# Recurrence gates as fp32 products in four quarters of the array, in place of three products on split operands

## The reference

```python
def lru_coeffs(xc, wa, ba, wx, bx, lam):
    xh = xc.reshape(B_, N, LRU_HEADS, LRU_HD)            # 8 heads of 64
    r = sigmoid(einsum('bnhi,hij->bnhj', xh, wa) + ba)
    i = sigmoid(einsum('bnhi,hij->bnhj', xh, wx) + bx)
    log_a = (-LRU_C * r) * softplus(-lam)
    a = exp(log_a)
    b = sqrt(-expm1(2.0 * log_a)) * (i * xc)
```

## Time and profile before

| | us |
|---|---|
| median of 3 runs | 797.6 |
| the profiled execution | 795.27 |
| its span, first to last instruction | 793.2 |
| TensorE busy | 740.0 |
| VectorE busy | 534.0 |
| ScalarE busy | 449.4 |
| GpSimd busy | 273.5 |
| mean granted clock of TensorE | 0.966 |

### The profile page before, as it was taken

The page is one execution under the profiler, slowest core; times in us unless marked ns, Lnnn a source line. Parts: engine busy times, 40 slices in busy tenths (PEclk is TensorE's granted clock), DMA queues, the critical chain, the costliest instruction groups (busy, mean ns, idle before and its releaser), DMA issues.

```text
span 793.2 us, 9934 instructions
## 1 busy us (share of the span) xinstructions
PE 740.0 (93%) x3468; PEld 602.5 (76%) x3468; DVE 534.0 (67%) x811; ACT 449.4 (57%) x743; POOL 273.5 (34%) x321
## 2 busy tenths in 40 slices
PE   3876989999999998999998999989999999999997
PEld 1575767888888877888887887758787888888885
DVE  4377654759997789788996655776645665766532
ACT  4266652798786975887984982334535133534311
POOL 0022335243435254224433456223211145443421
PEclk9596999999999998999999999989999999999999
DMA  9998003334355245344453134344458667967531
GB/s 363 347 324 242 27 28 107 93 97 117 116 181 173 64 157 173 99 126 137 163 167 112 58 104 142 98 146 147 115 197 305 224 209 252 307 214 264 180 114 76
DMA packets 89218, 130.11 MB, mean 164 GB/s; under 512 B 22768, under 2 KB 54128, under 8 KB 87632
## 3 DMA queue, kind: packets, MB, share of 16 engines
q1 hardware_dynamic: 84800, 115.44, 45.0%
q0 software_dynamic: 4368, 14.03, 6.4%
HBM read 91.17 MB, written 38.27 MB: 163 GB/s over the span
## 4 chain that ended last, share of the span: by engine, by line
PE 72%; DVE 8%; issue 6%; DMA 5%; ACT 5%; POOL 3%; SPq 1%; DVEq 0%; ACTq 0%; POOLq 0%
PE bank L1543 23%; PE bank L1545 23%; PE bank L1544 23%; DMA wm<-in_w_mod 3%; DVE xg L1186 1%; ACT bank L878 1%; ACT fbuf L895 1%; POOL xTh L609 1%; DVE xTl L1194 1%; DMA pv<-scratch_u 1%; PE bank L1579 1%; DVE xg L1166 1%; DMA wraw<-in_w_in 1%; PE bank L1669 1%; PE bank L1559 0%
## 5 line engine op out<-in xcount | busy, mean ns | idle before, releaser
L1543 PE MATMUL bank<-xTh,wh 128*128 128x512 f32 (+1 forms) x592 | 237.0, 400 | 7.4 <-DVE xTl L1194 4.0
L1545 PE MATMUL bank<-xTh,wl 128*128 128x512 f32 (+1 forms) x592 | 231.3, 391 | 0.0
L1544 PE MATMUL bank<-xTl,wh 128*128 128x512 f32 x576 | 226.9, 394 | 0.0
L1543 PEld LDWEIGHTS bank<-xTh,wh 128*128 128x128 f32 x592 | 112.8, 190 | 32.9 <-DVE xTl L1194 5.7
L1545 PEld LDWEIGHTS bank<-xTh,wl 128*128 128x128 f32 x592 | 112.5, 190 | 23.5
L1544 PEld LDWEIGHTS bank<-xTl,wh 128*128 128x128 f32 x576 | 109.8, 191 | 22.5 <-issue 1.2
L1543 PE MATMUL bank<-xTh 128*128 128x512 f32 (+1 forms) x272 | 104.2, 383 | 1.9 <-issue 1.4
L1544 PE MATMUL bank<-xTl,xTh 128*128 128x512 f32 x256 | 99.6, 389 | 0.0
L1545 PE MATMUL bank<-xTh,xTl 128*128 128x512 f32 x256 | 99.6, 389 | 0.0
L911 ACT ACTIVATE ustage<-bank 128x512 f32<-128x512 f32 x56 | 33.0, 593 | 92.3 <-PE bank L1545 75.9
L609 POOL TENSOR_SCALAR sph<-xc 128x512 fp32r<-128x512 f32 (+1 forms) x36 | 26.9, 762 | 122.1 <-PE bank L1545 67.5
(11 more groups left out here) (192 smaller groups left out, 1428.8 us busy)
## 6 DMA issues: line engine op xcount, KB each, us to landing
scratch_u<-ustage SPq DMA_DIRECT2D x72, 256.0 KB, 3.2
wraw<-in_w_in SPq DMA_DIRECT2D x18, 512.0 KB, 5.2
wm<-in_w_mod SPq DMA_DIRECT2D x8, 1024.0 KB, 14.4
xg<-in_x SPq DMA_DIRECT2D x16, 512.0 KB, 9.2
yb<-scratch_y SPq DMA_DIRECT2D x32, 256.0 KB, 3.6
gb<-scratch_u SPq DMA_DIRECT2D x32, 256.0 KB, 5.0
xres<-in_x SPq DMA_DIRECT2D x16, 512.0 KB, 4.7
out<-tout SPq DMA_DIRECT2D x15, 512.0 KB, 3.0
```

Source lines behind the costliest of these rows:

```text
L1543: mm(out, wh_, xh_, start=first, stop=False)
L1544: mm(out, wh_, xl_, start=False, stop=False)
L1545: return mm(out, wl_, xh_, start=False, stop=last)
```

## The change

The gates are no longer made from split operands. Each gate is two fp32 products: one for each head, with 64 rows and 64 columns of the array, from `gwr` (the weights as they are loaded) and `xc` itself. With top for partitions 0 to 63 and low for 64 to 127, the decay gate uses the quarters top-top and low-low, the input gate the two others: top input goes to low output and the other way round. ScalarE's sigmoid of the input gate writes each half to the other half of `Ib`, as two instructions of 64 partitions. The split tiles, their splits on GpSimd and VectorE, the zeroing of the block-diagonal weights and their semaphores go; the layout of the memory behind them is kept by skipping as many bytes. Gate weights are loaded into two buffers in turn. The convs of VectorE stand elsewhere: `conv(here + 4)` behind `one_minus_a2` of s = 1 (before: at the end of s = 0), `conv(after + 1)` at the end of s = 3 (before: at the start of s = 4).

```diff
@@ mixer_kernel, tiles
-        sph = a3.take("sph", [P, 2, CH], f32r)
-        spl = a3.take("spl", [P, 2, CH], f32r)
-        gwh = a3.take("gwh", [P, 4, P], f32r)
-        gwl = a3.take("gwl", [P, 4, P], f32r)
-        gwr = a3.take("gwr", [P, 4, 64])
+        gwr = a3.take("gwr", [P, 2, 4, 64])
+        a3.off += 4 * (4 * CH + 2 * 4 * P - 4 * 64)
@@ GpSimd
             def load_gate_w(t):
-                if t:
-                    pool.wait_ge(s_gwl, 2 * t)
-                g.dma_start(gwr[:], gate_w[t]).then_inc(s_gw, 16)
+                if t >= 2:
+                    pool.wait_ge(s_pg, (NCH + 1) * (t - 1))
+                g.dma_start(gwr[:, t % 2], gate_w[t]).then_inc(s_gw[t % 2], 16)
@@
-            gate_w_hi(0)
-            split(0)
@@
-                if s == NCH and more:
-                    gate_w_hi(t + 1)
-                if q + 1 < STEPS:
-                    split(q + 1)
@@
-                if s == NCH and more:
+                if s == NCH - 1 and more:
                     load_v(after + 2)
@@ ScalarE, sigmoids(q)
-                    a.activation(Ib[:, d, 0:n], gi_[d][:, 0:n], ACT.Sigmoid,
-                                 bias=par_col("lru_bx", 4 * d + t)).then_inc(s_sig, 1)
+                    for h, other in ((slice(0, 64), slice(64, 128)), (slice(64, 128), slice(0, 64))):
+                        a.activation(Ib[h, d, 0:n], gi_[d][other, 0:n], ACT.Sigmoid,
+                                     bias=par_col("lru_bx", 4 * d + t)[h]).then_inc(s_sig, 1)
@@ VectorE
-            gate_w_lo(0)
-            split_lo(0)
             conv(1)
@@
-                if s == NCH and t + 1 < N_LRU:
-                    gate_w_lo(t + 1)
-                    conv(after + 1)
                 for j in convs_in_step(q, 4):
                     conv_glu(j)
                 one_minus_a2(q)
-                if q + 1 < STEPS:
-                    split_lo(q + 1)
+                if s == 1:
+                    conv(here + 4)
@@
                 if s == 0:
                     conv(here + 3)
-                    conv(here + 4)
                 if s == 2 and t + 1 < N_LRU:
                     conv(after)
+                if s == NCH - 1 and t + 1 < N_LRU:
+                    conv(after + 1)
@@ TensorE, gates(q)
                 if s == 0:
-                    pe.wait_ge(s_gwl, 2 * t + 2)
-                pe.wait_ge(s_sl, splits_before(q + 1))
+                    pe.wait_ge(s_gw[t % 2], 16 * (t // 2 + 1))
+                pe.wait_ge(s_cv, (NCH + 1) * t + LAST_PIECE[s] + 1)
                 if q:
-                    pe.wait_ge(s_sig, 4 * q)
+                    pe.wait_ge(s_sig, 6 * q)
                     pe.wait_ge(s_m2, 2 * q)
-                for m in range(4):
-                    d = 0 if s == 0 else m // 2
-                    b = gi_[m // 2] if m % 2 else gr[m // 2]
-                    ins = mm3(b[:, 0:n], gwh[:, m, :], gwl[:, m, :], sph[:, d, 0:n], spl[:, d, 0:n], True, True)
+                w, top, low = gwr[:, t % 2], slice(0, 64), slice(64, 128)
+                for d, c in enumerate(step_chunks(s)):
+                    x = xc_piece(t, c)
+                    mm(gr[d][top, 0:n], w[top, 2 * d], x[top], start=True, stop=True)
+                    mm(gr[d][low, 0:n], w[low, 2 * d], x[low], start=True, stop=True)
+                    mm(gi_[d][low, 0:n], w[top, 2 * d + 1], x[top], start=True, stop=True)
+                    ins = mm(gi_[d][top, 0:n], w[low, 2 * d + 1], x[low], start=True, stop=True)
                 ins.then_inc(s_pg, 1)
```

More of the change, by code:

```diff
@@ L97, in convs_in_step @@
     return [g for g in range(N_CONV) if GATES_AFTER[q] <= CONV_AT[g] - lead < STEP_END[q]]
-def splits_before(q):
-    t, s = divmod(q, NCH + 1)
-    return (2 * NCH + 1) * t + (2 * s - 1 if s else 0)
 def mixer_kernel(nc, x, ctx, par, w_mod, b_gate, g_post, w_in, gate_w, pool_w, conv_dw, conf_pw, w_out,
@@ L285, in mixer_kernel @@
         s_us = [sem(f"u_stored{b}") for b in range(U_SLOTS)]
-        s_gz, s_gw, s_gwh, s_gwl = sem("gatew_zeroed"), sem("gatew_in"), sem("gatew_hi"), sem("gatew_lo")
+        s_gw = [sem(f"gatew_in{b}") for b in range(2)]
         s_v, s_cv = [sem(f"v_in{b}") for b in range(2)], sem("convolved")
-        s_sh, s_sl, s_pg, s_sig = sem("split_hi"), sem("split_lo"), sem("gates_done"), sem("sigmoids")
+        s_pg, s_sig = sem("gates_done"), sem("sigmoids")
         s_aq, s_exp, s_m2, s_rt = sem("a_and_q"), sem("tanhs"), sem("one_minus_a2"), sem("roots")
@@ L629, in _ @@
             pool.wait_ge(s_hl, 8 * (NCH + 1))
-            g.memset(gwh[:].bitcast(f32), 0.0).then_inc(s_gz, 1)
-            g.memset(gwl[:].bitcast(f32), 0.0).then_inc(s_gz, 1)
             g.memset(czl[:].bitcast(f32), 0.0).then_inc(s_czero, 1)
@@ L654, in load_v @@
                     g.dma_start(vbuf[:, p % 2, off:off + b - a], u_dram[V_LRU + t, :, a:b]).then_inc(s_v[p % 2], 16)
[L656 to L674, removed]
             def gated_input(q):
@@ L680, in gated_input @@
                 for d, c in enumerate((f, b)):
-                    pool.wait_ge(s_sig, 4 * q + d + 3)
+                    pool.wait_ge(s_sig, 6 * q + 2 * d + 4)
                     I = Ib[:, d, 0:n]
@@ L931, in decays @@
                     kc = 4 * d + t
-                    act.wait_ge(s_sig, 4 * q + d + 1)
+                    act.wait_ge(s_sig, 6 * q + d + 1)
                     if s == 0 and t or s == 4:
@@ L1248, in _ @@
             lo_group(NCH)
[L1250 to L1254, removed]
             def conv(p):
@@ L1339, in conv_w_lo @@
                 v.tensor_tensor(out=cwl[:, b], in0=cwraw[:, b], in1=cwh[:, b].bitcast(f32), op=ALU.subtract).then_inc(s_cwlo, 1)
[L1341 to L1349, removed]
             w_lo(4)
```

## The result

The changed kernel takes 807.25 us (median of 4 runs, 805.2 to 807.62), the kernel before beside it 797.15: a ratio of 1.0131, 95% interval 1.0109 to 1.0152. It is slower by 10 us, where 16.6 us less were forecast. The profiled execution took 807.36 us, with a span of 805.4.

A forecast was written before the change was run, and what follows sets the result against it. TensorE was taken to bound the recurrence steps. Gates net of switching 15.4, gap 5.2, less lateness 2 and conv 2, save 16.6 us: 795.3 to 778.7, plus 2.3 for the median, 781; range 774 to 800.

The forecast's parts named there:

- What bounds: In the stage of the 20 recurrence steps TensorE sets the pace, with 319.09 us of work in 327.
- the quarters: TensorE's gate products: four quarters run side by side, a long step takes 1.71 us, not 2.78; 19.4 us saved before switching.
- the switching: TensorE's array changes tiling into and out of every step, 40 times: 0.1 us each, 4 us (0 to 7.6).
- rival (a): Gate quarters on TensorE take turns: 27.8 us slower, 825, or 74 us slower, 872, if nothing overlaps; chance 0.15 for both.
- the lateness: ScalarE runs late in steps with only two projections because of the added half sigmoids: 2 us lost (0 to 6).
- the signs: Named as showing it wrong: dearer half-height PSUM reads, gates waiting for late ScalarE in more than three steps, or growing gaps.
- Rival (b): ScalarE's lateness carries from step to step and gates wait for `one_minus_a2`: 10 us back, 792; chance 0.13.
- The gap of step 9: TensorE's 4.33 us wait before the second conv unit shrinks to 1.5; with full clock behind it, 5.2 us gained (0 to 6.7).
- conv(here + 4): On VectorE behind `one_minus_a2` of the first long step, it delays the second's gates in tiles 0 and 2: 2 us lost.

The follow-up runs named there:

- the first experiment: The changed kernel with the input gate's sigmoid as one instruction on 128 partitions for each direction, uncrossing left out: 776.07 us, ratio 0.9734 to the kernel before.

## Why the prediction was wrong

**What bounds, and the quarters: right, with the switching too small.** Four quarters run side by side, and rival (a) is refuted by the four starts above. But the gates with their switching cost 2.77 - 3 x 0.23 = 2.08 us a long step, against four slots of 0.43, 1.71. So switching is 0.36 us a step, 7 us in all, where the sum had 4 (0 to 7.6). Net 12 us are saved, forecast 15.4. The Trainium skill ("TensorEngine Tiling (Array Packing)", Restrictions and Gotchas, on PSUM pressure) says that different row tiles cannot access the same bank simultaneously. Read by bank alone, this is at odds with the trace: L1568 and L1569 lie in different rows of the array, write one bank in different partitions, and start together. By the 3.07 of the Trainium skill ("TensorE: Matmul & The Clock Gate", section on packing small matmuls) a long step would take 2.23 us, an estimate, in which the prediction took the switching to be included; the trace has 2.08, which is 6.86/2.08 = 3.3 times, or 6.86/1.87 = 3.7 without what lies outside the gates.

**ScalarE: the step that failed.** The prediction said that an added half sigmoid costs between nothing and 0.58 us, and that 2 us (0 to 6) were to be put on the lateness. The added two cost 1.7 us a step instead of 1.15: in this order the halves do not overlap one another. And the lateness cost 31 us, as the first experiment shows, in place of 2.

Two arguments made it look small. The first was load against length over the stage (278 in 311). That is a mean, and it holds only if ScalarE could work while it waits; but its waits for transfers (31 us for stores here), for TensorE's next unit and for `one_minus_a2` are fixed in its order of instructions. The second was that lateness is used up in the longer steps. In the kernel before, the sigmoids begin at most 1.4 us behind the start of the product that follows the gates. With one sigmoid a direction this lag grows to 0.1, 1.5 and 2.9 us in steps 11, 12 and 13, and the longer way to step 14 brings it back to 0.1. In the changed kernel it is 1.1, 2.7 and 5.2 in the same steps, and then 4.3, 5.7 and 3.2 in steps 14 to 16: the longer way takes off only 0.9 us. Step 13, where the projection behind the gates starts at 360.40 in the changed kernel and at 343.89 with one sigmoid:

```profile
365.63 1.24 ACT L883 ACTIVATE bank<-bank,prm 128x512 f32<-128x512 f32 x2
```

```profile
346.76 1.24 ACT L883 ACTIVATE bank<-bank,prm 128x512 f32<-128x512 f32 x2
```

The rows had the answer. In the steps with two projections ScalarE counted 15 to 16 us against TensorE's 14.6, which is a deficit, and it was read as a small one. Two of the signs that the prediction named for being wrong appeared: gates waited for `one_minus_a2` in four steps, and a gap grew, that of step 16. About 10 of the 31 us come from the two staging slots, as the runs with three show: an evacuation behind time makes its store late, and that one holds up the evacuation after the next.

**Rival (b)** named the mechanism, with 10 us where it has 26 (781 to 807), and with too small a chance.

**The gap of step 9.** Right in its cause and in the size of the gap (1.55 us with the conv moved alone, 1.5 forecast). The gain was too small by the clock: full speed came back behind both gaps, and the move gives 7.5 us instead of 5.2. In the changed kernel it was eaten again: ScalarE's Tanh is late there too, and the gap stands at 3.3 us.

**conv(here + 4).** Forecast 2 us, measured 5 by putting it back. The waits for `xc` are 3.3 us, at steps 2 and 12 as forecast; the rest is the gap of step 16, where the prediction kept it at 3.2:

```profile
432.50 0.55 PE L1487 MATMUL bank<-cvzh,cvwh 128*128 128x256 f32 x1 [6.14 <-issue]
```

This gap needs both causes: it is 2.5 us with the conv back and 1.3 us with one sigmoid and the conv still moved.

**The parts in a row.** Five of the kernels differ from one to the next by one part of the change or nearly so. From before (796.6 beside it) to the conv of s = 4 moved (789.0) it is - 7.5, forecast - 5.2. To the quarters with DMA copies (774.6) it is - 14.5, forecast - 15.4 for the quarters alone. To the quarters without copies and with `conv(here + 4)` moved (776.1) it is + 1.5, forecast + 2. To the changed kernel, which adds only the half sigmoids (807.3), it is + 31, forecast + 2. So the last term alone turns the forecast round. The second and the last difference compare kernels timed apart, so the parts sum to + 10.7 where + 10.1 was measured.

## What to carry to other kernels

Before work is moved onto an engine that isn't the bound, add it to that engine's own chain for one period of the loop, its fixed waits included, and compare that with the shortened period of the engine that is relieved; a share of busy time over the stage can't show this. If an operand must change partitions, try a DMA on the input, where it has time, before an engine that reads the output in the loop: here that was the difference between 774.6 and 802.1 us. And where an engine starts to run late, look for the small ring of buffers that turns its lateness into more.

## What the runs showed that had not been expected

Instructions of ScalarE on 64 partitions and 512 elements take 0.68 us, about as long as on 128 (0.69). Two of them in a row start 0.58 us apart if both write the same half, and 0.71 apart if they write different ones, even when each reads and writes its own half (0.71 in the run with uncrossed halves too, 2.81 us for four). Four fp32 products in four quarters, two of them into one bank from different rows of the array, start within 0.02 us, and the change of tiling costs 0.36 us a step in all: 0.32 from the product ahead to the first group where 0.23 is usual, 0.48 to the second group where 0.43 is usual, 0.54 from the start of the last group (327.77) to 328.31, and 0.34 from there to the next product where 0.23 is usual.
